# Three norms beside latent attention: sums as columns of tokens, inverse roots spread by a product with diagonals

## What is computed

```
y_mla  = mla_mixer(...)                  # 8 heads of latent attention, 512 channels
y_conv = silu(layernorm(conv(u), g, b))  # 31 taps, 256 channels
y_hy   = hyena_mixer(...)                # long convolutions, 256 channels
y = concatenate([rmsnorm(y_mla, g[:512]), rmsnorm(y_conv, g[512:768]), rmsnorm(y_hy, g[768:])])
x = x + y @ w_out
```

## Time and profile before

| | us |
|---|---|
| median of 3 runs | 3206.03 |
| lowest, highest | 3203.32, 3206.67 |
| the profiled execution: its time | 3206.92 |
| its span | 3205.1 |
| attention, layer 0: first to last slot | about 565 to 659 |
| attention, layer 1 | about 1616 to 1710 |
| TensorE busy over the span | 3042.6 (95%) |
| VectorE | 1616.5 (50%) |
| ScalarE | 722.4 (23%) |
| GpSimd | 1894.7 (59%) |

### The profile page before, as it was taken

How to read it: one execution, slowest core, us unless ns; L and a number is a source line. 1 busy time by engine, 2 the same in 40 slices (tenths; PEclk the granted TensorE clock), 3 DMA queues, 4 the chain that set the end, 5 groups by cost and what they waited for, 6 DMA issues and landing times.

```text
span 3205.1 us, 38602 instructions
## 1 busy us (share of the span) xinstructions
PE 3042.6 (95%) x14016; PEld 2360.7 (74%) x14016; DVE 1616.5 (50%) x2411; ACT 722.4 (23%) x1403; POOL 1894.7 (59%) x2079
## 2 busy tenths in 40 slices
PE   6999999989999999999998999989999999999998
PEld 4887866568888788776756788857777666678786
DVE  4424488843213532357984421246743888652514
ACT  2101022631001110111263100124432444320101
POOL 5867763047767777676403776745654333377876
PEclk9999999989999999999999999989999999999999
DMA  4322322012323222231301232214231111122322
GB/s 129 102 84 97 110 74 76 1 53 85 112 82 118 79 97 96 94 110 65 97 1 40 86 115 82 100 65 140 79 108 66 47 40 43 40 87 96 107 80 75
DMA packets 79547, 261.20 MB, mean 81 GB/s; under 512 B 16063, under 2 KB 19327, under 8 KB 78881
## 3 DMA queue, kind: packets, MB, share of 16 engines
q1 hardware_dynamic: 61344, 238.86, 22.3%
q10 hardware_dynamic: 18048, 20.27, 2.1%
HBM read 257.00 MB, written 2.10 MB: 81 GB/s over the span
## 4 chain that ended last, share of the span: by engine, by line
PE 84%; DVE 9%; POOL 2%; ACT 2%; issue 2%; DMA 0%; ACTq 0%; DVEq 0%; SPq 0%; POOLq 0%
PE psum L588 23%; PE psum L590 23%; PE psum L589 23%; POOL w_lo L557 2%; PE psum L787 1%; PE psum L938 1%; PE psum L803 1%; PE psum L865 1%; PE psum L807 1%; PE psum L805 1%; PE psum L710 1%; DVE rinv L1947 1%; DVE mx L2271 1%; PE psum L928 1%; DVE prob L2318 1%
## 5 line engine op out<-in xcount | busy, mean ns | idle before, releaser
L557 POOL TENSOR_TENSOR w_lo<-w_raw,w_hi 128x256 fp32r<-128x256 f32 (+2 forms) x1660 | 1421.5, 886 | 34.6
L552 POOL TENSOR_SCALAR w_hi<-w_raw 128x1024 fp32r<-128x1024 f32 (+2 forms) x415 | 473.4, 1141 | 1253.5 <-PE psum L590 731.1
L588 PE MATMUL psum<-u_hi,w_hi 128*128 128x512 f32 x2368 | 942.1, 398 | 24.0 <-POOL w_lo L557 8.1
L589 PE MATMUL psum<-u_lo,w_hi 128*128 128x512 f32 x2368 | 927.2, 392 | 0.0
L590 PE MATMUL psum<-u_hi,w_lo 128*128 128x512 f32 x2368 | 926.9, 391 | 0.0
L588 PEld LDWEIGHTS psum<-u_hi,w_hi 128*128 128x128 f32 x2368 | 448.1, 189 | 145.5 <-issue 44.2
L589 PEld LDWEIGHTS psum<-u_lo,w_hi 128*128 128x128 f32 x2368 | 448.5, 189 | 94.2 <-issue 3.8
L590 PEld LDWEIGHTS psum<-u_hi,w_lo 128*128 128x128 f32 x2368 | 447.8, 189 | 94.9
L588 PE MATMUL psum<-h_hi,w_hi 128*128 128x512 f32 x960 | 374.7, 390 | 3.4 <-issue 3.4
L590 PE MATMUL psum<-h_hi,w_lo 128*128 128x512 f32 x960 | 373.6, 389 | 0.0
L589 PE MATMUL psum<-h_lo,w_hi 128*128 128x512 f32 x960 | 373.5, 389 | 0.0
(11 more groups left out here) (335 smaller groups left out, 3391.4 us busy)
## 6 DMA issues: line engine op xcount, KB each, us to landing
w_raw<-in_w SPq DMA_DIRECT2D x335, 512.0 KB, 3.3
w_raw<-in_w SPq DMA_DIRECT2D x48, 768.0 KB, 4.2
w_raw<-in_w SPq DMA_DIRECT2D x32, 640.0 KB, 3.9
w_c<-in_w_c ACTq DMA_DIRECT2D x2, 2048.0 KB, 9.0
x<-in_xt SPq DMA_DIRECT2D x1, 2048.0 KB, 8.2
decay<-in_decay ACTq DMA_DIRECT2D x16, 128.0 KB, 3.7
dft<-in_dft ACTq DMA_DIRECT2D x8, 256.0 KB, 4.5
idft<-in_idft ACTq DMA_DIRECT2D x4, 512.0 KB, 6.1
```

Of the source, the lines that this page charges most:

```text
L552: pool.tensor_scalar(hi, raw, 1.0, 1.0, ALU.mult, ALU.mult).then_inc(w_hi_ready, 1)
L557: ins = pool.tensor_tensor(lo[:, part], raw[:, part], hi[:, part].bitcast(F32), ALU.subtract)
L588: pe.matmul(out, hi[:, c, :], rhs_hi(c), start=(s == 0), stop=False)
L589: pe.matmul(out, hi[:, c, :], rhs_lo(c), start=False, stop=False)
```

## The change

`sums_as_columns` takes the place of `sums_of_squares` for the three norms. The squared tile's blocks of 128 tokens are now the weights and one column of `ones` streams, so the bank holds 128x4: one partition per token of a block, one column per block. For two tiles that is eight matmuls of one column in place of two of 512. ScalarE takes the root of 128x4 into `root4`, VectorE inverts 128x4 into `inv4` in one instruction, and ScalarE writes four diagonal blocks `diag[:, t, :]`, each the identity times a column of `inv4` (`diagonals`). TensorE multiplies `ones` by the 128x512 of `diag` (`spread`): every partition of bank 3 gets the 512 inverse roots. `scaled` reads them there in place of `rinv`.

By slot: diagonals on ScalarE in 15, 22 and 34; spreads on TensorE in 17, 24 and 35; inversions on VectorE in 14, 22 and 33; scaling of `hy` in 18 and 19 in place of 19 and 20. The sums of slot 20 now wait for both scalings of `hy` (they read bank 3), and those of slot 31 for both scalings of the layernorm.

```diff
+                def sums_as_columns(out):
+                    for c in range(2):
+                        pe.wait_ge(sq_ready, w.sq + 1)
+                        for t in range(TB):
+                            mm = pe.matmul(out[:, t:t + 1], sq[w.sq % 2][:, P * t:P * t + P], ones[:, 0:1],
+                                           start=(c == 0 and t == 0), stop=(c == 1), skip_group_check=True)
+                        mm.then_inc(sq_used, 1)
+                        w.sq += 1
+                def spread(i, out):
+                    pe.wait_ge(diag_in, 3 * layer + i)
+                    pe.matmul(out[:, :], ones[:, :], diag[:, :, :].rearrange("p t n -> p (t n)"), start=True, stop=True,
+                              skip_group_check=True).then_inc(spread_done, 1)
...
                     elif s == 20:
-                        pe.wait_ge(root_in, 4 * layer + 1)
-                        sums_of_squares(banks[3])
+                        pe.wait_ge(u_full, w.full + 2)
+                        sums_as_columns(banks[3])
...
+                    elif s in (17, 24, 35):
+                        spread((17, 24, 35).index(s) + 1, banks[3])
...
+                def diagonals():
+                    roots[0] += 1
+                    act.wait_ge(inverse_in, roots[0])
+                    act.wait_ge(spread_done, roots[0] - 1)
+                    for t in range(TB):
+                        ins = act.activation(diag[:, t, :], ident[:, :], ACT.Copy, scale=inv4[:, t:t + 1])
+                    ins.then_inc(diag_in, 1)
...
                     elif s == 13:
-                        deviation(banks[3][:, :], sq0 + 2, HYC)
+                        act.wait_ge(rinv_ready, w.norm)
+                        columns_root(banks[3], sq0 + 2, HYC)
+                    elif s in (15, 34):
+                        diagonals()
...
                 def scaled(tile, gain):
-                    return dve.scalar_tensor_tensor(tile, tile, gain, rinv[:, :], ALU.mult, ALU.mult)
+                    return dve.scalar_tensor_tensor(tile, tile, gain, banks[3][:, :], ALU.mult, ALU.mult)
-                def inverted(i, quarter):
-                    part = slice(P * quarter, P * quarter + P)
-                    if quarter == 0:
-                        dve.wait_ge(root_in, 4 * layer + i)
-                        dve.wait_ge(u_full, w.full)
-                        dve.wait_ge(vec_ready, w.vec)
-                    ins = dve.reciprocal(rinv[:, part], std[:, part])
-                    if quarter == 3:
-                        ins.then_inc(rinv_ready, 1)
-                        w.norm += 1
+                def inverted(i):
+                    dve.wait_ge(root_in, 4 * layer + i)
+                    dve.wait_ge(diag_in, 3 * layer + i - 1)
+                    dve.reciprocal(inv4[:, :], root4[:, :]).then_inc(inverse_in, 1)
```

More of the change, by code:

```diff
@@ L199, in build @@
         htmp = [place(f"htmp{i}", [P, T], F32, TMP_AT + (9 + i) * KB2) for i in range(2)]
+        diag = place("diag", [P, TB, P], F32, TMP_AT + 2 * KB2)
+        root4, inv4 = (place(name, [P, TB], F32, TMP_AT + 3 * KB2 + 64 * e) for e, name in enumerate(("root4", "inv4")))
         cosq = place("cosq", [P, T], F32, ROPE_AT)
@@ L387, in build @@
         mean_done = sem("mean_done")
+        inverse_in = sem("inverse_in")
+        diag_in = sem("diag_in")
+        spread_done = sem("spread_done")
         root_in = sem("root_in")
@@ L1037, in beside_slot @@
                     elif s == 31:
-                        pe.wait_ge(root_in, 4 * layer + 2)
-                        sums_of_squares(banks[3])
+                        pe.wait_ge(vec_ready, v0 + 15)
+                        sums_as_columns(banks[3])
+                    elif s in (17, 24, 35):
+                        spread((17, 24, 35).index(s) + 1, banks[3])
                     elif s == 33:
@@ L1056, in half @@
                     if begin == 0:
+                        if (w.m + j) % 4 == 3:
+                            pe.wait_ge(u_full, w.full - 4)
                         pe.wait_ge(w_split, n + 1)
@@ L1649, in deviation, with columns_root @@
                     w.norm += 1
+                def columns_root(src, used, dim):
+                    act.wait_ge(sq_used, used)
+                    act.wait_ge(inverse_in, roots[0])
+                    act.activation(root4[:, :], src[:, 0:TB], ACT.Sqrt, scale=1.0 / dim, bias=col("eps", None, 0))\
+                        .then_inc(root_in, 1)
+                def diagonals():
+                    roots[0] += 1
+                    act.wait_ge(inverse_in, roots[0])
+                    act.wait_ge(spread_done, roots[0] - 1)
+                    for t in range(TB):
+                        ins = act.activation(diag[:, t, :], ident[:, :], ACT.Copy, scale=inv4[:, t:t + 1])
+                    ins.then_inc(diag_in, 1)
+                roots = [3 * layer]
                 def high(c, src, full_at):
@@ L1676, in beside_slot @@
                     elif s == 21:
-                        deviation(banks[3][:, :], sq0 + 4, CONVC)
+                        columns_root(banks[3], sq0 + 4, CONVC)
                     elif s in (22, 23):
@@ L1680, in beside_slot @@
                         high(s - 16, hy[:, s - 18, :], w.full + s - 21)
+                        if s == 22:
+                            diagonals()
                     elif s in (24, 25):
@@ L1693, in beside_slot @@
                     elif s == 32:
-                        deviation(banks[3][:, :], sq0 + 8, CONVC)
+                        columns_root(banks[3], sq0 + 8, CONVC)
                 attention(mla_units(), beside_slot)
@@ L1699, in mixer @@
                     high(4 + t, y_conv[:, t, :], w.full + 3 + t)
+                act.wait_ge(spread_done, 3 * layer + 3)
                 deviation(banks[5][:, :], w.sq, 512)
@@ L2513, in beside_slot @@
                         convolve(1)
-                    elif s in (14, 15, 17, 18):
-                        inverted(1, (14, 15, 17, 18).index(s))
+                    elif s == 14:
+                        inverted(1)
                     elif s == 16:
@@ L2539, in mixer @@
                 w.act += 8
-                dve.wait_ge(rinv_ready, w.norm)
+                dve.wait_ge(spread_done, 3 * layer + 3)
                 dve.wait_ge(act_ready, w.act)
```

16 lines of the change are left out of this document (8 added, 8 removed).

## The result

| | before | after |
|---|---|---|
| median of the runs, us | 3206.15 (6 runs) | 3219.16 (6 runs) |
| lowest, highest | 3203.32, 3207.39 | 3217.92, 3220.5 |
| span of the profiled execution | 3205.1 | 3217.4 |
| ratio to before, 95% interval | | 1.0041 [1.0031, 1.0051] |

The change costs 13 us, 0.4%. The forecast was 3208.8, with a range up to 3214, so it was wrong in size and in its verdict of no change.

What follows compares the result with a forecast made beforehand. Most slots were taken as set by TensorE's own queue, those around a root by ScalarE. Terms 0.9 + 0.4 + 0.1 gave +1.4 us a layer, +2.8 for both: median 3208.8, range 3199 to 3214.

Steps and rivals of the forecast that it cites:

- VectorE's relief: Attentions: 24 quarter inversions, 22.2 us of VectorE's time, go; counted at nothing, as hidden by TensorE's queue and ScalarE.
- Rival A: Attention slots: VectorE was the pace after all, 6.6 us a layer saved, 13.2 in all, 3192.8; chance 0.07.
- Slot 12: First sums by columns in the attention: a set takes some 2.1 us against 1.72, plus 0.4.
- Slots 13 to 20: Root, diagonals and spread: lag about -0.2 at the scores of unit 16, +0.7 at 18, +0.2 at 20.
- Diagonals: ScalarE, slots 15, 22 and 34: about 0.40 us each, four in 1.2, bounds 0.8 and 1.6; free in slot 15.
- the shorter root: ScalarE's root of 128x4 in place of 128x512: 0.39 us saved in slot 13 and again in slots 21 and 22.
- the upper bound of diagonals and spreads on the path: Each on the path at 1.6 and 0.86, three times, less the two roots: 6 us a layer at most.
- Slots 21 and 22: Exponential of unit 22 about 0.3 earlier, then 1.2 us of diagonals ahead of unit 23's; lag becomes +0.9.
- Slot 31, sums by columns again: +0.4: Late in the attention, the third set by columns again adds 0.4 us to the lag.
- the granted clock in the last 15 us of the attention: Sign at an attention's end: the forecast is wrong if TensorE's granted clock there differs from before.
- Rival B: Slot 31's columns and products behind run at half clock: +2.1 and +1.0, 9.0 us in all, 3215; chance 0.13.
- Rival C: Before slot 31 and the last projection chunks, less TensorE idling shrinks half-speed stretches: -10 and +2.8, 3198.8; chance 0.05.

Runs made afterwards that it cites:

- wide128_dve_b: Second measurement of `wide128` with the diagonals written by VectorE in one instruction in place of four on ScalarE: 3203.33 us, 0.9995 of the kernel before.
- nodiag: `wide128` without diagonals, the spread made of four products with a repeated `inv4` column as weights and the identity streaming: 3206.03 us, 1.0002 of the kernel before.
- wide128: The changed kernel with 128 columns of ones streamed in place of one in all three sets: 3207.84 us, 1.0009 of the kernel before.
- refill: The changed kernel with an unread fp32 product of 508 columns directly behind the sets of slots 20 and 31: 3213.75 us.
- wide8: The changed kernel with 8 columns of ones streamed in place of one in all three sets: 3216.87 us.
- dve21: `wide128_dve_b` with the set of slot 20 moved to the end of slot 21: 3219.61 us.
- no_sums: The kernel before with the sums of slots 20 and 31 left out, so its result is wrong: 3203.47 us.
- before_col: The kernel before with a set of one-column products, result overwritten, added ahead of the sums of slots 20 and 31: 3208.39 us.

## Why the prediction was wrong

What held, all lags from slot 12 and against the prediction's own:
- VectorE's relief wins nothing that these lags show: the inversions by quarters were hidden. After, VectorE idles for TensorE instead (1.03 us ahead of 618.74, 2.68 ahead of 622.88). Rival A is out.
- Slot 12: +0.4 was expected of a set; it costs nothing at full clock. 595.99 to 597.69 is 1.70, against 1.72 before; in slot 20 it is 1.81. That is 0.11 an instruction, less than the 0.135 of the earlier trace rows. The 0.025 that the Trainium skill's page "TensorE: Matmul & The Clock Gate" gives in its section "Back-to-back issue gap" is, by the words of that section, a gap with no budget for weight loads. So it was no forecast for these matmuls, each of which has a load of new weights, and the prediction was right to expect the row to hold.
- Slots 13 to 20: -0.34 at the scores of unit 16 (-0.2 expected), +0.63 at unit 18 (+0.7), +0.16 at unit 20 (+0.2), +0.41 at unit 21 (+0.85: the wait ahead of the sums was 0.16, not 0.25, and the set 0.3 shorter).
- Diagonals: four in 1.27, 394 ns each (1.2 and 0.40 expected). On the path they cost about 0.5. And without them on ScalarE the lag at unit 25 is +0.14 to +0.19, where the shorter root was to make it -0.3 (`wide128_dve_b`, `nodiag`). So the price of the diagonals and the gain of the root were both too high, and the errors partly cancel. The diagonals of slot 22:

```profile
626.49 1.27 ACT L1688 ACTIVATE diag<-ident,inv 128x128 f32<-128x128 f32 x4
```

- Rid of the clock's fall, the lag is +0.70 at unit 25 in `wide128`, where +0.9 was expected. Its 3207.84 is also near the 3208.8 of the sum, but that is partly luck: at the projection the lag is -0.07 in layer 0 and +2.46 in layer 1, where +1.4 was the sum for each, and 1.9 of the 2.46 is the idle time without a releaser, of which the prediction knew nothing.
- Two figures of the prediction don't follow from its own terms, and nothing hangs on them: the upper bound of diagonals and spreads on the path is (1.6 + 0.86) x 3 less twice 0.39, 6.6 a layer and not 6, and the bounds 3204 to 3212.4 are given without their sum.

What failed is the step **"Slots 21 and 22"**, and behind it **"Slot 31, sums by columns again: +0.4"**. Both took TensorE's clock as given while its queue was full. One of the prediction's own signs says so: the granted clock in the last 15 us of the attention was not to differ from before, and it is 0.55 in place of 1.00 in 652 to 661. At the scores of unit 25 the lag was +2.10 instead of +0.9: the exponential of unit 22 was to be 0.3 earlier, but ScalarE waited for transposes at half clock:

```profile
623.38 0.60 ACT L1497 ACTIVATE pt<-psum 128x512 f32<-128x512 f32 x1 [1.30 <-PE psum L728]
```

In slots 31 to 35 it was +3.47 instead of +0.5. Rival B had this place, the doubled loads and the doubled products behind them, and with its +3.1 on top of the 0.5 it would say 3.6 for these slots, against 3.47. The 1.2 more of slots 21 and 22 it didn't have. And it made the fall hang on how long ScalarE's table loads had kept TensorE waiting, so it got 0.13. That the columns themselves keep the clock from coming back, or bring it down where nothing waits, was no rival. Rival C's mechanism is real and small: in layer 0 of `wide128` the clock comes back earlier at slot 31 (0.73 against 0.57 in 646 to 652), and from the scores of unit 31 to the set are 4.14 us in place of 4.77. In layer 1 they are 4.76, as before.

Shown: the loss is the clock's (the widened sets keep every instruction and its place, and give 11.3 of 13 us back; the idle 1.9 of layer 1 stays in what is left), and each of the two places has half of it, this by one execution of each variant. Shown too: the set alone isn't enough; long products next to it, or another slot, keep the clock in many executions. Open: which property of the stretch decides. The sets differ from the old sums both in few streamed columns and in sixteen loads in a row, and only the first was varied; a plain wait of the same length in the same place wasn't tried. In `refill` and `wide8` the same instructions lose the clock behind slot 20 in layer 0 and keep it in layer 1, so their order alone doesn't decide. Open as well is the 1.54 us of issue in layer 1; nothing in the traces names its cause.

## What to carry to other kernels

A matmul with few streamed columns and new weights cost 0.11 us an instruction here, with 1 column as with 32, and beside that it can cost the clock of what runs behind it. Before summing over partitions into columns this way, try letting each product stream more columns than are needed: 128 cost under 0.1 us a set here and kept the clock, 32 kept it too, and 8 did not in every place. When a change puts narrow matmuls into TensorE's queue, read the granted clock ahead of them and behind them, and price the stretch behind at both levels, even if the queue never idles. And compare the clock over the whole span, not only where the edit is: `dve21` lost 10 us in a block that it doesn't touch, nearly as much as the clock's fall in the attention cost, and its delay alone doesn't explain that. Before putting such a loss down to a shift in time, look for another trace that has the same shift.

## What the runs showed of the hardware

- A full queue did not keep TensorE's clock: 6.00 of 6 us busy at a granted clock of 0.72 (after), against 3.81 busy at 1.00 (`no_sums`).
- Sixteen fp32 instructions with new weights take 1.70 to 1.81 us from start to start with one streamed column, and 1.78 to 1.89 with 128.
- The same code, started at 2334.59, ran at half clock for some 20 us in `dve21` (2340 to 2355: 0.50), some 600 us behind the nearest edited code, and at 1.00 in `before_col` (2334.72) and `wide128` (2334.10).
- The same instructions in the same order kept the clock in one layer and lost it in the other (`wide8` behind slot 20: 0.72 in layer 0, 1.00 in layer 1).
- Weights read with one column repeated 128 times are no slower than others: a spread of eight such instructions takes 0.89.
